# One low part on GpSimd, three rectifications ahead of the value rows, and the first queries turned one half unit sooner

## The reference

```python
u = jnp.einsum('bsd,de->bse', a, w_in[i])
q, k, v, qi, ki, wi, u_conv, u_pool = jnp.split(u, IN_SPLITS_2, axis=-1)
q = partial_rope(q...); k = partial_rope(k...)           # the first 16 of 64 columns of a head
qi = partial_rope(qi...); ki = partial_rope(ki...)
y_attn = dsa_sparse_attention(q, k, v, qi, ki, wi)
#   idx = einsum(relu(qi . ki), wi) * scale, causal; the 64 largest of each row are kept
#   softmax(q . k) over the kept keys, times v, for 8 heads
y_conv = conformer_conv(u_conv, ...)    # a * sigmoid(g), 31 taps, layer norm, silu, 256x256 product
y_pool = multiscale_pool(u_pool, ...)   # means over 2, 4, 8, 16 tokens, minus the input
mix = jnp.concatenate([y_attn, y_conv, y_pool], axis=-1) @ w_out[i]
```

## Time and profile before

| | |
|---|---|
| median of 3 executions | 1879.25 us (1879.14 to 1880.73) |
| the profiled execution | 1880.8 us, its span in the trace 1879.0 us |
| PE busy | 1854.1 us (99%) |
| DVE busy | 1342.0 us (71%) |
| ACT busy | 1001.7 us (53%) |
| POOL busy | 127.1 us (7%) |
| GpSimd's two working stretches | about 1211 to 1293 us and 1554 to 1636 us |

### The profile page before, as it was taken

The page is one execution under the profiler, slowest core; times in us unless marked ns, Lnnn a source line. Parts: engine busy times, 40 slices in busy tenths (PEclk is TensorE's granted clock), DMA queues, the critical chain, the costliest instruction groups (busy, mean ns, idle before and its releaser), DMA issues.

```text
span 1879.0 us, 36714 instructions
## 1 busy us (share of the span) xinstructions
PE 1854.1 (99%) x15946; PEld 1840.6 (98%) x15946; DVE 1342.0 (71%) x1661; ACT 1001.7 (53%) x1251; POOL 127.1 (7%) x110
## 2 busy tenths in 40 slices
PE   8999999999999999999999999999999999899998
PEld 8999999999999999999999999999999999899998
DVE  7755788785558755788776556888866688787566
ACT  6444555564447544546564445867543467664434
POOL 1000000000000000000000000263000005600000
PEclk9999999999999999999999999999999999999999
DMA  8556555565554655555556555523565644047552
GB/s 268 205 188 202 170 151 170 167 204 188 193 202 163 225 193 189 182 159 173 178 170 202 187 195 172 180 91 95 182 214 189 204 128 154 29 159 244 194 189 68
DMA packets 246531, 329.55 MB, mean 175 GB/s; under 512 B 6246, under 2 KB 218788, under 8 KB 246372
## 3 DMA queue, kind: packets, MB, share of 16 engines
q1 hardware_dynamic: 246018, 326.79, 52.8%
q0 software_dynamic: 96, 0.26, 0.1%
q10 hardware_dynamic: 258, 0.16, 0.0%
HBM read 326.14 MB, written 1.05 MB: 174 GB/s over the span
## 4 chain that ended last, share of the span: by engine, by line
PE 91%; DVE 5%; ACT 3%; issue 1%; DMA 0%; DVEq 0%; ACTq 0%
PE work L2121 21%; PE work L2122 21%; PE work L2123 21%; PE acc L2121 9%; PE acc L2122 9%; PE acc L2123 9%; ACT w_hi L802 1%; DVE w_lo L1355 1%; PE work L2307 1%; DVE fa L1818 1%; PE acc L2223 1%; DVE fa L1894 0%; ACT cs L1088 0%; DVE small L1891 0%; DVE ra L1368 0%
## 5 line engine op out<-in xcount | busy, mean ns | idle before, releaser
L1355 DVE TENSOR_TENSOR w_lo<-raw,w_hi 128x2048 fp32r<-128x2048 f32 (+1 forms) x308 | 681.8, 2215 | 91.2 <-ACT w_hi L802 91.0
L2121 PE MATMUL work<-x_rows,w_hi 128*128 128x256 f32 x2560 | 710.0, 277 | 0.9 <-DVE x_rows L1389 0.7
L2122 PE MATMUL work<-x_rows,w_hi 128*128 128x256 f32 x2560 | 705.9, 276 | 0.0
L2123 PE MATMUL work<-x_rows,w_lo 128*128 128x256 f32 x2560 | 705.8, 276 | 0.0
L802 ACT ACTIVATE w_hi<-raw 128x2048 fp32r<-128x2048 f32 (+2 forms) x313 | 579.0, 1854 | 163.4 <-PE work L2123 68.9
L2121 PEld LDWEIGHTS work<-x_rows,w_hi 128*128 128x128 f32 x2560 | 482.0, 188 | 2.0 <-DVE x_rows L1389 1.2
L2122 PEld LDWEIGHTS work<-x_rows,w_hi 128*128 128x128 f32 x2560 | 481.9, 188 | 0.3
L2123 PEld LDWEIGHTS work<-x_rows,w_lo 128*128 128x128 f32 x2560 | 481.8, 188 | 0.0
L2121 PE MATMUL acc<-ra,w_hi 128*128 128x256 f32 x1352 | 372.4, 275 | 0.0
L2122 PE MATMUL acc<-ra,w_hi 128*128 128x256 f32 x1352 | 372.0, 275 | 0.0
L2123 PE MATMUL acc<-ra,w_lo 128*128 128x256 f32 x1352 | 372.0, 275 | 0.0
(11 more groups left out here) (322 smaller groups left out, 2245.3 us busy)
## 6 DMA issues: line engine op xcount, KB each, us to landing
raw<-in_ffn_w_gu_dram SPq DMA_DIRECT2D x88, 1024.0 KB, 5.1
raw<-in_w_in_dram SPq DMA_DIRECT2D x52, 1024.0 KB, 5.4
raw<-in_ffn_w_down_dram SPq DMA_DIRECT2D x44, 1024.0 KB, 5.0
raw<-in_w_up_dram SPq DMA_DIRECT2D x32, 1024.0 KB, 5.5
raw<-in_w_down_dram SPq DMA_DIRECT2D x32, 1024.0 KB, 4.9
raw<-in_w_mla_out_dram SPq DMA_DIRECT2D x8, 1024.0 KB, 5.4
raw<-in_w_o_dram SPq DMA_DIRECT2D x8, 1024.0 KB, 5.4
raw<-in_w_ple_gate_dram SPq DMA_DIRECT2D x8, 1024.0 KB, 5.2
```

The costliest lines, as they stand in the source:

```text
L1355: v.tensor_tensor(w_lo[:, s, 0:n], raw[:, r, 0:n], w_hi[:, s, 0:n].bitcast(F32), ALU.subtract).then_inc(lo_done.sem, 1)
L2121: pe.matmul(dst, ah, bh, start=start and i == 0, stop=False, skip_group_check=not group)
L2122: pe.matmul(dst, ah, bl, start=False, stop=False, skip_group_check=not group)
L2123: last = pe.matmul(dst, al, bh, start=False, stop=stop and i == len(pairs) - 1, skip_group_check=not group)
```

## The change

- GpSimd makes the low part of chunk Q2 + 1 between taps 9 and 10 (`low_part`), and VectorE's `next_lo(here, KV2)` goes. The next low part that VectorE makes waits for it (`lo_done` in `half_of_lo`).
- ScalarE's `relus(3)` stands ahead of the value and key rows, where it stood behind them.
- TensorE turns the first queries between the two token halves of ("q",1), where it turned them behind both. So ("qt",0) is now unit 16 and ("q",1) unit 17.
- VectorE makes `queries_lo(0)` in round 6, ahead of the rotation of the second queries, where it made it in round 7.

```diff
-    names += [("q", 0), "kt", ("q", 1), ("qt", 0), ("sc", 0), ("sc", 1), ("qt", 1)]
+    names += [("q", 0), "kt", ("qt", 0), ("q", 1), ("sc", 0), ("sc", 1), ("qt", 1)]
@@ gpsimd
+                def low_part(c):
+                    at = CHUNK_AT[here] + c
+                    gp.wait_ge(hi_done.sem, at + 1)
+                    gp.wait_ge(lo_done.sem, at)
+                    gp.tensor_tensor(w_lo[:, at % RING, :], raw[:, at % RAWS, :], w_hi[:, at % RING, :].bitcast(F32),
+                                     ALU.subtract).then_inc(lo_done.sem, 1)
...
                 for j in range(1, TAPS_FIRST + 1):
                     tap(j)
+                    if j == 9:
+                        low_part(Q2 + 1)
@@ scalar
                 keys_values = bank2(U2["kv"])
+                relus(3)
                 act.wait_ge(*vec_out.at(here, ("rope", "kv")))
...
                 last.then_inc(part_hi.event(here, "kd"), 1)
-                relus(3)
@@ vector
                 rope_unit("kv", "kv", 2)
-                next_lo(here, KV2)
                 values_lo()
...
                     if r == 6:
+                        queries_lo(0)
                         rope_unit(("q", 1), "q1")
-                    if r == 7:
-                        queries_lo(0)
...
                     v.wait_ge(hi_done.sem, at + 1)
+                    v.wait_ge(lo_done.sem, at)
@@ tensor
-                def by_token(c, unit):
+                def by_token(c, unit, between=None):
                     free(here, U2[unit])
                     w = weights(here, c)
                     for tb in range(TB):
+                        if tb and between is not None:
+                            between()
                         last = token_half(c, unit, tb, w)
...
-                by_token(Q2 + 1, ("q", 1))
-                pe.wait_ge(*unit_taken.at(here, U2["q", 0]))
-                turned(("qt", 0), tm[:, 0, :, :])
+                def first_queries():
+                    pe.wait_ge(*unit_taken.at(here, U2["q", 0]))
+                    turned(("qt", 0), tm[:, 0, :, :])
+
+                by_token(Q2 + 1, ("q", 1), first_queries)
```

## The result

| | before | after |
|---|---|---|
| median of 11 executions | 1879.96 us (1878.78 to 1881.76) | 1884.21 us (1881.92 to 1885.65) |
| ratio | | 1.0019, 95% interval 1.0011 to 1.0026 |
| the profiled execution | 1880.8 us, span 1879.0 us | 1884.21 us, span 1882.4 us |
| PE busy | 1854.1 us | 1852.6 us |
| mean granted clock | 0.996 | 0.998 |

A forecast was written before the change was run, and what follows sets the result against it. TensorE was taken as the bound, busy 1854.1 of 1879.0 us. Layer 0's -0.7 and layer 1's +1.0 us made +0.3: 1881.1 us for the profiled execution, 1879.5 us in the median, range 1872.5 to 1883.2 us.

The forecast's parts named there:

- The subtraction on GpSimd: GpSimd's new low part of chunk 9 takes 4.5 us, from about 1240.8 to 1245.3, hidden in GpSimd's idle time.
- What it does to VectorE: VectorE's addition of rotated keys waits until GpSimd's subtraction ends: near 1245.5 instead of 1241.31, about 4.4 us long.
- first rival: VectorE is not held by GpSimd's subtraction: landmarks 2.9 and 3.3 us earlier, 1873.0 us; chance 0.18 for both layers.
- the hold: VectorE's addition of rotated keys blocked at the shared SBUF ports for GpSimd's whole subtraction, 4.5 us; chance 0.62 in both layers.
- `weighted(3)` 3.5 us late: Behind ScalarE's rows and the values' low part, VectorE's `weighted(3)` starts at 1247.4 instead of 1243.95.
- Their move is worth nothing here: ScalarE's rectifications, moved ahead of the value and key rows, are ready in either order: no gain.
- Layer 0, 0.7 us gained: Layer 0: rounds end 2.3 us late, but the earlier turning brings the first turning of probabilities to 1271.8, 0.7 us sooner.
- landmark: The first turning of probabilities in each layer, at 1272.52 and 1615.71 before; its shift measured each layer's gain or loss.
- Layer 1, 1.0 us lost: Layer 1: 4.2 us late, none swallowed; TensorE waits 1.7 and 3.4 us, clock partly low, landmark at 1616.7.
- So I carry a shift of the landmark unchanged to the end: Behind each layer's landmark the engines do as before, so its shift reaches the program's end unchanged.
- third rival: Turning the first queries sooner does nothing by itself; counted inside the forecast, with no chance of its own.
- new waits behind the landmark: A sign that would prove the forecast wrong: further waits after the first turning of probabilities, set at none.

The follow-up runs named there:

- e5: The changed kernel with GpSimd's subtraction cut into four pieces of 512 columns, one signal behind the last: 1877.00 us, 0.9985 of the kernel before.
- e4: The whole change, with GpSimd's subtraction also waiting for the rotation of the keys: 1877.08 us, 0.9981 of the kernel before.
- e6: The kernel before with only `relus(3)` moved ahead of the value and key rows: 1883.21 us, ratio 1.0012.
- e2: The kernel before with the low part on GpSimd between taps 9 and 10, no reordering: 1887.58 us, ratio 1.0037.
- e7: e4 with the third rectification put back behind the value and key rows: 1877.80 us, 0.9983 of the kernel before.
- e1: The changed kernel with the low part back on VectorE, the three reorderings kept: 1877.86 us, 0.9983 of the kernel before.
- e3: The kernel before with only the earlier turning of the first queries and `queries_lo(0)` in round 6: 1877.29 us, ratio 0.9982.
- e8: e1 with five idle maxima, about 3.0 us, on VectorE ahead of the rotation of the keys: 1882.79 us, 1.0009 of the kernel before.

## Why the prediction was wrong, step by step

**The subtraction on GpSimd: right.** 4.51 and 4.63 us, predicted 4.5. Start 1241.07, predicted 1240.8.

**What it does to VectorE: right.** 4.38 and 4.50 us, predicted 4.4. The rule of the Trainium skill on which I had weighed this (SBUF — State Buffer, "Who interferes with whom": a lock that the first has while the other is fully blocked) agrees with this case: L1799 takes 4.38 and 4.50 us, and ends 0.09 us behind the subtraction in layer 0. And e5 shows that it ends with the instruction. The first rival was refuted for the changed kernel. GpSimd answered the signal 0.14 us late and won the race. The rival's mechanism ("VectorE is not held") is e4 in effect. Between the two I had 6.5 us, and 7.1 lie between the medians of e4 and the changed kernel, so the price of the hold was nearly right.

**`weighted(3)` 3.5 us late: right.** +3.44 and +3.58 us at the low part of the values.

**"Their move is worth nothing here": right for the changed kernel.** Its third rectification ends at 1242.81, and the value rows start at 1245.71, behind the hold:

```profile
1242.23 0.58 ACT L1086 ACTIVATE acc<-acc 128x512 f32<-128x512 f32 x1 [0.70 <-PE acc L2132]
1245.71 0.62 ACT L1167 ACTIVATE vp<-work,cols 128x128 fp32r<-128x128 f32 x2 [2.90 <-DVE work L1799]
```

Without a hold the value rows do wait for it. In the old order the move costs 2.3 us (e6), most of it in additions that come to lie beside GpSimd; beside the earlier turning nothing that can be told.

**Layer 0, 0.7 us gained: wrong, 0.19 lost.** Up to the rotated first queries the sum held: they start 17.16 us behind the last index products, before 14.93, so 2.23 us late, where 3.9 - 1.66 makes 2.24. Behind them lies the miss of 0.9 us, mainly in additions that take longer beside GpSimd, which I didn't look for. On GpSimd the taps and pool sums had moved with the delay, and the rotated first queries went from 0.30 to 0.72 us, the second from 0.53 to 0.96: 0.85 us. I had priced such a meeting at L1874 alone, where +0.29 came of the expected 0.4. Another 0.17 us lie between first mask and landmark (2.37 us, where my sum had 2.2).

```profile
1259.77 0.72 DVE L1799 TENSOR_TENSOR work<-fa 128x128 f32<-128x128 f32 x1
1267.48 0.96 DVE L1799 TENSOR_TENSOR work<-fa 128x128 f32<-128x128 f32 x1
```

One pause that I hadn't expected doesn't show in the 2.23 us. From the values to L1883 it is 4.83 us, before 4.47. VectorE shows a pause of 0.50 us there in layer 0 of every kernel with the low part on GpSimd (after, e2, e4, e5, e7), and in none of the others. In layer 1 of these kernels the same stretch is 4.47 or 4.48. The kernel before has such pauses of VectorE at other places (0.52 us at 1580.10, 0.50 at 1298.01), so it may have moved here with the order of the instructions. What it waits for I can't tell from the rows.

**Layer 1, 1.0 us lost: right in sum (0.99), with one step wrong.** The waits of 1.7 and 3.4 us were 1.50 and 3.25. The clock did not fall behind them as I had assumed: it was 1.00 in all of 1600 to 1650, before 0.93. I had put the time with the clock up at 0.6 us less. Against it stands L1799 of the second queries, 0.96 us where before it took 0.30.

```profile
1600.00:1650.00 50.00, 41.50 (x320) 1.00 0.10 31
```

**"So I carry a shift of the landmark unchanged to the end": the step that failed.** The landmarks moved by +0.19 and +0.99 us, 1.2 together, and the end by 3.4. Against the forecast of +0.3 us that is 3.1 too much: 2.0 arise behind the landmarks, where I had set nothing, 0.9 in front of layer 0's, and 0.2 ahead of the stretch. Of the 2.0, 0.9 lie between landmark and third mask (0.43 and 0.45), 0.36 between third mask and mean (0.33 and 0.03), and 0.72 between the layers.

What the landmark leaves out is VectorE's own queue behind the rounds: two masks with their maxima, `queries_lo(1)`, the low part of the pool sums, and only then the third mask. Before, in layer 0, this queue had room:

```profile
1271.54 0.69 DVE L1368 TENSOR_TENSOR ra<-work,ra 128x512 fp32r<-128x512 f32 x1
1272.15 0.68 DVE L1363 TENSOR_TENSOR ra<-fa,ra 128x512 fp32r<-128x512 f32 x1
1273.77 0.56 DVE L1461 SCALAR_TENSOR_TENSOR fa<-work,fa 128x384 f32<-128x384 f32 x1 [0.87 <-PE work L2123]
```

and after, none:

```profile
1272.80 0.68 DVE L1378 TENSOR_TENSOR ra<-work,ra 128x512 fp32r<-128x512 f32 x1
1273.40 1.22 DVE L1373 TENSOR_TENSOR ra<-fa,ra 128x512 fp32r<-128x512 f32 x1
1274.62 0.53 DVE L1471 SCALAR_TENSOR_TENSOR fa<-work,fa 128x384 f32<-128x384 f32 x1
```

The stretch from first to third mask was 4.72 and 5.20 us before. It is 4.05 in both layers after, and 4.05 or 4.06 in e1, e3, e4, e5, e7 and e8: VectorE's instructions end to end, without a pause. One of them is held by GpSimd, by the same amount in both layers of all seven kernels: the low part of the pool sums takes 1.22 or 1.23 us, where 0.68 is its undisturbed length. GpSimd's multiplication has started 0.36 to 0.38 us ahead of it each time. After, in layer 0:

```profile
1273.03 1.04 POOL L752 TENSOR_TENSOR fa<-fa,vecs 128x512 f32<-128x512 f32 x1
```

The multiplication ends at 1274.07 and L1373 at 1274.62, 0.55 us later. Without this 0.54 us the stretch would be about 3.5 us, an estimate, if TensorE has the third scores ready by then. So the earlier turning takes 1.1 and 1.6 us out of the landmark (from the first mask it is 2.37 us, before 3.47 and 3.97), and only 0.67 and 1.15 out of what follows. Each layer gave back 0.4 us this way, less than the 0.54 us of the hold, and TensorE waits 0.57 us for L1373.

The third mask would have been the better landmark. From it to the mean it is 21.2 or 21.3 us in both layers of all ten kernels, except where the granted clock falls in this stretch (six places, 21.55 to 22.62).

Then the clock. Behind layer 0's landmark it now falls where it did not before:

```profile
1280.00:1284.00 4.00, 4.00 (x25) 0.62 0.01 4
```

25 matmuls in 4 us, before 37 at 1.00. Such a drop stood before at 1268 to 1272 (0.68), so it has moved and not come on top. Yet from third mask to mean it costs 0.33 us (21.55 for 21.22), and in e8, which falls between 1272 and 1280, 1.15 us (22.37). Of the 0.72 us between the layers, 0.62 arise at one place, at the norm at the layer's end. Until 1320.32 before and 1321.50 after, TensorE's instructions are 1.18 us apart; the next product that others wait for starts at 1321.48 and 1323.28, 1.80 us apart. In front of it stand five products by zero (`warm`) that the kernel puts into the wait, before and after:

```profile
1320.79 0.84 PE L2130 MATMUL work<-rot_r,zero_r 128*128 128x256 f32 x5
1322.06 1.42 PE L2139 MATMUL work<-rot_r,zero_r 128*128 128x256 f32 x5
```

Before, they run at a granted clock of 1.00 (1320.79 to 1321.48) and the clock falls behind them, to 0.55 until 1324.35. After, it is already down, at 0.50 from 1322.06 to 1323.28. So the drop lies a little sooner after, and the five products ahead of the awaited one take 0.24 us each and not 0.14. Whether the change does that, one execution of each can't show. e1, e3, e4 and e7 have no drop there, e5, e6 and e8 have one in front of the product as well.

**What the same failed step did to the first rival.** I gave 6.2 us of gain to a kernel without the hold. e4 gains 0.19%, 3.6 us: its means are 2.21 and 1.91 us sooner, for predicted 2.9 and 3.3. The forecast and this rival are both too fast: by 3.3 us and by 2.6 us, if the measured ratios are set on 1880 us (+3.6 for +0.3, and -3.6 for -6.2). The error was not in the hold of the rotated keys, on which all chances were spent, but in what is left of the earlier turning behind the landmark. In the third rival I had also priced it too low beside the hold: without it "layer 0 would lose about 0.7 more". Without the orders (e2) the means are 1.60 and 2.56 us later than in the changed kernel.

**Chances and range.** I had "new waits behind the landmark" as what would prove it wrong, and gave it no room in the range.

## What to carry to other kernels

Before work is moved to GpSimd, look at which two-input VectorE instruction starts beside it. One short addition on the critical chain, caught for a whole 4.5 us instruction, cost 7 us here, and one wait for an event that was there anyway, or four shorter instructions, took all of it back. A landmark for a sum has to count the queues of all engines that the delay passes through: here VectorE's queue behind it was the longer one, with a hold of 0.54 us in it, and each delay ahead also moved GpSimd's instructions onto VectorE's next additions. When an instruction is moved ahead of another, look for its own wait, and for what the shift puts side by side: the rectification was free behind the hold, and cost 2.3 us in the old order (e6).

## What was not expected of the hardware

- TensorE's clock stayed at its upper level through the waits of layer 1 (1.50, 3.25 and 0.89 us; 1.00 from 1600 to 1650), while before one wait of 4.35 us in the same stretch ended in 0.50. In e7 it stayed at 1.00 from 1200 to 1872, and its profiled execution is the shortest of the ten (1876.45 us). Those of e1, e3 and e4, with one drop each in these layers, took 1877.85, 1877.40 and 1879.07. The medians of the four kernels (1877.1 to 1877.9) can't be told apart, and one trace of each doesn't show whether such a drop belongs to the kernel or to the execution.
- The clock also fell where TensorE had paused only shortly: between 1316 and 1328 it is below 1.00 in six of the ten traces, where TensorE's only waits since 1300 were 0.22 and 0.64 us, around matmuls of one column. The other four have the same waits and no drop.
- VectorE's low parts of values and its weighted sums, which read `work` and `acc`, ran their usual 0.61 and 2.14 us beside a GpSimd instruction of 4.54 us (e4). The lengthened instructions shown in this document all read from two operands in SBUF (`fa`, `consts`, `ra`), none of them `work` or `acc`.
